# Bringing the experts' rows back amid the last expert's products, and turning rows behind the branch

## The reference, cut to what matters

```python
for l in range(2):
    h = x @ w_in[l]                       # 1892 columns; three kinds of attention follow
    x = layer_norm(ALPHA * x + mix @ w_out[l], ln1_g[l], ln1_b[l])
    x = layer_norm(ALPHA * x + moe_ffn(x, ...), ln2_g[l], ln2_b[l])

def moe_ffn(x, ...):                      # each row: one group of 4 experts, two experts in it
    h = silu(x @ w_gate[e]) * (x @ w_up[e]) * gates[:, e]
    return sum over e of h @ w_down[e]
```

## Time and profile before

| | |
|---|---|
| runs (us) | 1201.88, 1197.25, 1195.83 |
| median | 1197.25 us |
| profiled execution | 1202.57 us, of which the span is 1201.2 us |
| mean granted TensorE clock | 0.974 of full speed |
| TensorE busy | 1130.9 us (94%) |
| VectorE, ScalarE busy | 906.5 us (75%), 732.6 us (61%) |

### The profile page before, as it was taken

How to read it: one execution, slowest core, us unless ns; L and a number is a source line. 1 busy time by engine, 2 the same in 40 slices (tenths; PEclk the granted TensorE clock), 3 DMA queues, 4 the chain that set the end, 5 groups by cost and what they waited for, 6 DMA issues and landing times.

```text
span 1201.2 us, 14612 instructions
## 1 busy us (share of the span) xinstructions
PE 1130.9 (94%) x5487; PEld 927.0 (77%) x5487; DVE 906.5 (75%) x1482; ACT 732.6 (61%) x1307; POOL 0.2 (0%) x4
## 2 busy tenths in 40 slices
PE   3999999999998999998999999999989999999996
PEld 2788888788777788887788788877768878787774
DVE  3657666677666876776578767999986876899996
ACT  4545565654646665556355454888855655488883
POOL 0000000000000000000000000000000000000000
PEclk9999999999998999999999897999999999899999
DMA  9455353453332464622542323999936332399991
GB/s 303 140 210 175 106 178 138 167 183 106 140 117 95 140 224 161 222 105 85 196 144 103 105 71 113 336 359 366 366 122 210 129 106 71 126 338 357 366 352 40
DMA packets 131554, 221.26 MB, mean 184 GB/s; under 512 B 6112, under 2 KB 77328, under 8 KB 131472
## 3 DMA queue, kind: packets, MB, share of 16 engines
q1 hardware_dynamic: 126128, 209.60, 50.6%
q10 hardware_dynamic: 5344, 10.60, 2.7%
HBM read 219.13 MB, written 1.05 MB: 183 GB/s over the span
## 4 chain that ended last, share of the span: by engine, by line
PE 77%; DVE 11%; ACT 9%; issue 2%; DMA 1%; SPq 0%; DVEq 0%; ACTq 0%
PE bank L483 21%; PE bank L485 20%; PE bank L484 20%; PE bank L775 3%; PE bank L840 3%; ACT wH L428 2%; ACT S L795 2%; DVE wL L436 2%; PE bank L631 1%; DVE mx L784 1%; PE bank L821 1%; PE bank L2212 1%; PE bank L1756 1%; DMA M<-in_mem 1%; PE bank L1689 1%
## 5 line engine op out<-in xcount | busy, mean ns | idle before, releaser
L436 DVE TENSOR_TENSOR wL<-ring,wH 128x1024 fp32r<-128x1024 f32 (+1 forms) x316 | 375.0, 1212 | 142.9 <-ACT wH L428 142.1
L428 ACT ACTIVATE wH<-ring 128x1024 fp32r<-128x1024 f32 (+1 forms) x316 | 320.1, 1047 | 26.9 <-PE bank L485 15.4
L483 PE MATMUL bank<-wH,hTH 128*128 128x512 f32 (+2 forms) x592 | 238.3, 403 | 6.0 <-issue 3.2
L485 PE MATMUL bank<-wH,hTL 128*128 128x512 f32 (+2 forms) x592 | 232.2, 392 | 0.0
L484 PE MATMUL bank<-wL,hTH 128*128 128x512 f32 (+2 forms) x592 | 232.0, 392 | 0.0
L483 PEld LDWEIGHTS bank<-wH,hTH 128*128 128x128 f32 x592 | 112.2, 190 | 29.9 <-issue 5.8
L485 PEld LDWEIGHTS bank<-wH,hTL 128*128 128x128 f32 x592 | 112.0, 189 | 24.1
L484 PEld LDWEIGHTS bank<-wL,hTH 128*128 128x128 f32 x592 | 112.3, 190 | 22.4 <-issue 0.5
L483 PE MATMUL bank<-wH,xgH 128*128 128x512 f32 x256 | 104.8, 409 | 0.0
L485 PE MATMUL bank<-wH,xgL 128*128 128x512 f32 x256 | 101.1, 395 | 0.0
L484 PE MATMUL bank<-wL,xgH 128*128 128x512 f32 x256 | 100.9, 394 | 0.0
(11 more groups left out here) (292 smaller groups left out, 1898.3 us busy)
## 6 DMA issues: line engine op xcount, KB each, us to landing
ring<-in_w_in_a SPq DMA_DIRECT2D x44, 1024.0 KB, 4.9
ring<-in_w_out SPq DMA_DIRECT2D x20, 1024.0 KB, 4.8
ring<-in_w_down SPq DMA_DIRECT2D x20, 1024.0 KB, 5.8
ring<-in_w_gate SPq DMA_DIRECT2D x36, 512.0 KB, 4.9
ring<-in_w_up SPq DMA_DIRECT2D x36, 512.0 KB, 6.0
ring<-in_w_in_b SPq DMA_DIRECT2D x14, 1024.0 KB, 5.0
ring<-in_w_mem_kv SPq DMA_DIRECT2D x8, 1024.0 KB, 6.3
ring<-in_w_in SPq DMA_DIRECT2D x8, 1024.0 KB, 5.2
```

Source lines behind the costliest of these rows:

```text
L428: act.e.activation(quarter_parts(q)[0], quarter_in_ring(q), COPY).then_inc(w_high, 1)
L436: dve.e.tensor_tensor(lo, quarter_in_ring(q), hi.bitcast(F32), SUB).then_inc(w_low, 1)
L483: pe.e.matmul(o, a[0], b[0], start=first, stop=False)
L485: return pe.e.matmul(o, a[1], b[0], start=False, stop=last)
```

## The change

In the way "few", for both layers:

- `back(1, 0, 2)`, eight matmuls, now comes behind down(14), ahead of turned(15); it writes row tile 1's sums into two banks of `att_bank` in place of banks 2 and 3, and `dve_added` gets these banks as `sums_in`. The index of `att_bank` is set to 3 ahead of up(15), so up(15) takes bank 4, turned(14) bank 5, and the two sums banks 6 and 7.
- `back(1, 2, 3)`, four matmuls, comes behind down(15), ahead of back(0, 3, 4); `back(1, 3, 4)` comes last.

In layer 0, TensorE's turning of row tile 0 (8 transposes) is moved out of both ways of the branch, to the front of the next layer's code (`pe_flip_x(0, "exit", ...)`), on a semaphore `first_normed`. ScalarE's and VectorE's part of it stays in the branch.

In layer 1, VectorE's order is added 0, middle 0, added 1, middle 1, scaled 0, scaled 1, and the store is four transfers of 128 x 512 in place of two of 128 x 1024.

```diff
             for c, x in enumerate(in_two(X[:, i, :])):
                 mm = dve.e.scalar_tensor_tensor(x, in_two(middle[i])[c], r[:, 0:1], lnw[:, 1, c * 512:(c + 1) * 512], MUL, ADD)
-                if key[-1] == 0 and i == 1:
-                    mm.then_inc(second_normed, 1)
+                if key[-1] == 0:
+                    mm.then_inc((first_normed, second_normed)[i], 1)
...
+        def act_flip_exit(way):
+            for j0 in (0, 4):
+                act.wait_ge(at("turned", "xT", "exit", 0, j0))
+                act.e.activation(hT[0][:, j0:j0 + 4, 0:P], bank_of["xT", "exit", 0, j0].t[:, :].rearrange("p (j n) -> p j n", j=4),
+                                 COPY).then_inc(*act.did("high", "exit", way, j0))
+
+        def dve_flip_exit(way):
+            for j0 in (0, 4):
+                dve.wait_ge(at("high", "exit", way, j0))
+                dve.e.tensor_tensor(hT[1][:, j0:j0 + 4, 0:P], bank_of["xT", "exit", 0, j0].t[:, :].rearrange("p (j n) -> p j n", j=4),
+                                    hT[0][:, j0:j0 + 4, 0:P].bitcast(F32), SUB).then_inc(first_turned, 1)
...
         def pe_mix_layer(l):
+            if l:
+                turn["att"] = 3
+                pe_flip_x(0, "exit", X, [(first_normed, 1), (first_normed, 2)])
             second = [at("added", "o1", 1, c) if l == 0 else (second_normed, c + 1) for c in range(2)]
...
-        def pe_finish(l, way):
-            if l == 0:
-                pe_flip_x(0, way, X, [at("x", *way, 0, c) for c in range(2)])
...
-        def dve_finish(l, way, ready):
-            for i in range(2):
-                dve_added(i, way, ready[i])
+        def dve_finish(l, way, ready, sums_in=(None, None)):
+            for i in range(2):
+                dve_added(i, way, ready[i], sums_in[i])
                 dve_middle(i, way, ln_loaded(l, 2))
-                dve_scaled(i, way)
-                if l == 0 and i == 0:
-                    dve_flip_x(0, way)
+                if l == 0:
+                    dve_scaled(i, way)
+                    if i == 0:
+                        dve_flip_exit(way)
+            if l:
+                for i in range(2):
+                    dve_scaled(i, way)
 
         def sp_finish(l, way):
             if l == 1:
                 for i in range(2):
-                    sp.wait_ge(*[at("x", *way, i, c) for c in range(2)])
-                    sp.e.dma_start(out[0, i * P:(i + 1) * P, :], X[:, i, :]).then_inc(d_out, 16)
+                    for c in range(2):
+                        sp.wait_ge(at("x", *way, i, c))
+                        sp.e.dma_start(out[0, i * P:(i + 1) * P, c * 512:(c + 1) * 512], X[:, i, c * 512:(c + 1) * 512]).then_inc(d_out, 16)
...
                     if g0 == 0:
-                        pe.wait_ge(b.free, at(*way, "OHT", i))
-                        b.free = at("added", *way, i, n)
+                        if i:
+                            b = att_bank((*way, "back", 1, n), at("added", *way, i, n))
+                        else:
+                            b = bank_of[(*way, "back", 0, n)] = banks[n]
+                            pe.wait_ge(b.free)
+                            b.free = at("added", *way, i, n)
+                        pe.wait_ge(at(*way, "OHT", i))
...
             for e in range(16):
                 g = e // 4
+                if e == 15:
+                    turn["att"] = 3
...
                 if e == 14:
                     back(0, 0, 1)
+                if e == 15:
+                    back(1, 0, 2)
             turned(15)
             back(0, 1, 3)
             down(15)
+            back(1, 2, 3)
             back(0, 3, 4)
-            back(1, 0, 4)
-            pe_finish(l, way)
+            back(1, 3, 4)
```

More of the change, by code:

```diff
@@ L377, in program @@
     d_x0 = sem("d_x0")
-    first_turned, second_normed = sem("first_turned"), sem("second_normed")
+    first_normed, first_turned, second_normed = sem("first_normed"), sem("first_turned"), sem("second_normed")
     d_mem, d_ln, d_u, d_late = [sem(f"d_mem{i}") for i in range(2)], sem("d_ln"), sem("d_u"), sem("d_late")
@@ L1568, in in_two, with dve_added @@
             return [row[:, c * 512:(c + 1) * 512] for c in range(2)]
-        def dve_added(i, key, ready):
+        def dve_added(i, key, ready, sums_in=None):
             sums, mean = small(2, "sums", i, *key), small(1, "mean", i, *key)
@@ L1573, in dve_added @@
                 dve.wait_ge(ready[c])
-                dve.e.scalar_tensor_tensor(x, x, ALPHA, banks[2 * i + c].t[:, :], MUL, ADD, accum_out=sums[:, c:c + 1]).then_inc(*dve.did("added", *key, i, c))
+                dve.e.scalar_tensor_tensor(x, x, ALPHA, (sums_in or banks[2 * i:2 * i + 2])[c].t[:, :], MUL, ADD, accum_out=sums[:, c:c + 1]).then_inc(*dve.did("added", *key, i, c))
             dve.follow().tensor_scalar(mean, sums[:, 0:1], sums[:, 1:2], -1.0 / D, ADD, MUL).then_inc(*dve.did("mean", i, *key))
@@ L1602, in pe_flip_x @@
             for c, j0 in enumerate((0, 4)):
-                b = att_bank(("xT", name, i, j0), (first_turned, c + 1) if name in (("few", 0), ("all", 0)) else at("xT", name, i, j0))
+                b = att_bank(("xT", name, i, j0), (first_turned, c + 1) if name == "exit" else at("xT", name, i, j0))
                 pe.wait_ge(ready[c])
@@ L1619, in dve_flip_x @@
                 dve.e.tensor_tensor(hT[1][:, j0:j0 + 4, i * P:(i + 1) * P], bank_of["xT", name, i, j0].t[:, :].rearrange("p (j n) -> p j n", j=4),
-                                    hT[0][:, j0:j0 + 4, i * P:(i + 1) * P].bitcast(F32), SUB).then_inc(
-                    *((first_turned, 1) if name in (("few", 0), ("all", 0)) else dve.did("xT", name, i, j0)))
+                                    hT[0][:, j0:j0 + 4, i * P:(i + 1) * P].bitcast(F32), SUB).then_inc(*dve.did("xT", name, i, j0))
+        def act_flip_exit(way):
[8 more added lines that the diff above has]
+                                    hT[0][:, j0:j0 + 4, 0:P].bitcast(F32), SUB).then_inc(first_turned, 1)
         def dve_rotate(src, dst, n, w, c, s, *name, scratch=T0):
@@ L2186, in act_finish @@
                 if l == 0 and i == 0:
-                    act_flip_x(0, way)
-        def dve_finish(l, way, ready):
+                    act_flip_exit(way)
+        def dve_finish(l, way, ready, sums_in=(None, None)):
             for i in range(2):
-                dve_added(i, way, ready[i])
+                dve_added(i, way, ready[i], sums_in[i])
                 dve_middle(i, way, ln_loaded(l, 2))
-                dve_scaled(i, way)
-                if l == 0 and i == 0:
-                    dve_flip_x(0, way)
+                if l == 0:
[5 more added lines that the diff above has]
+                    dve_scaled(i, way)
         def sp_finish(l, way):
@@ L2246, in back @@
                 for n in range(2):
-                    b = banks[2 * i + n]
                     if g0 == 0:
-                        pe.wait_ge(b.free, at(*way, "OHT", i))
-                        b.free = at("added", *way, i, n)
+                        if i:
[5 more added lines that the diff above has]
+                        pe.wait_ge(at(*way, "OHT", i))
+                    b = bank_of[(*way, "back", i, n)]
                     for g in range(g0, g1):
@@ L2384, in dve_few @@
             down(15)
-            dve_finish(l, way, [[at(*way, "back", i, n) for n in range(2)] for i in range(2)])
+            dve_finish(l, way, [[at(*way, "back", i, n) for n in range(2)] for i in range(2)],
+                       [[bank_of[(*way, "back", i, n)] for n in range(2)] for i in range(2)])
         def experts(l):
@@ L2428, in write @@
             experts(l)
-        sp.wait_ge((d_out, 32))
+        sp.wait_ge((d_out, 64))
     def lanes(engines):
```

## The result

| | before | changed |
|---|---|---|
| median of 22 runs each (us) | 1198.70 | 1203.76 |
| lowest and highest | 1194.20, 1204.67 | 1196.49, 1209.71 |
| profiled execution's span | 1201.2 | 1201.7 |

The ratio changed to before is 1.0037, with a 95% interval of 1.0022 to 1.0052: 0.37% or 4.4 us slower (2.6 to 6.2). That is within the 0.5% bound and within the range of 1195.0 to 1205.0 us; it is 5 us above the 1198.7 that before had beside it. The profiled pair shows only 0.5 us between the spans, because the profiled execution of the changed kernel was already 2.8 us ahead when it came to the first changed place, in code that is the same. So I compare stretches: from VectorE's start on expert 15's hidden values in layer 0 to ScalarE's second copy of h10 (L551, tile 1), and from the same instruction in the last layer to the span's end.

A forecast was written before the change was run, and what follows sets the result against it. TensorE was taken as busy for 94% of the span, with 77% of the chain. Layer 0's +1.15 and the last layer's +0.85 gave +2.0 us on 1197.25, so 1199.3 us; range 1195.0 to 1205.0.

The forecast's parts named there:

- Part 1: back(1, 0, 2) ahead of turned(15): its eight matmuls delay down(15) by 1.6 us in layer 0, 1.85 in the last.
- Part 2: back(1, 2, 3) behind down(15): four matmuls, 0.93 us, in a 1.4 us TensorE gap; no cost, no gain.
- Part 3: Layer 0's transposes behind the branch: h10 starts 0.9 us earlier, then waits for the fourth quarter's split; layer 0 costs +1.15.
- Part 4: Last layer's VectorE order: shift of 1.85 us less 0.35 of waits for ScalarE's root, so +1.5 us.
- Part 5: Last layer's store by halves: less data behind the last half row, -0.65 us, bounds 0 and -0.9.
- the halved store gives nothing: Rival, chance 0.08: the last transfer's time is mostly not data; +2.65 us, 1199.9.
- A gain at the exit: Rival, chance 0.16: ScalarE's and VectorE's branch-exit stalls shrink, h10's start decides; layer 0 -0.85 us, total 1197.3.
- TensorE's exit is longer: Rival, chance 0.12: leaving layer 0's branch exceeds 3.24 us, delaying tile 0's transposes; +1.1 us, 1200.4.
- A half clock at the wrong time: Rival, chance 0.06: TensorE's half clock falls at 905, on h10's last k steps, for 17 us; +9.8, 1207.0.

The follow-up runs named there:

- e1: Kernel before with only the order of the bringing back (back matmuls) changed, transposes, last layer's order and store kept; ratio to before 1.0025.
- e3: Changed kernel with the fourth quarter of h10 split within the branch, beside down(15); ratio to before 1.0007.
- e2: Changed kernel with before's order of back matmuls, tile 1's sums sharing a bank with tile 0's turned rows, so overwritten; ratio to before 1.0016.
- e4: Kernel before with only the last layer's store in four transfers; ratio to before 0.9993.
- f3: Changed kernel with VectorE's last-layer order as before: added, middle, scaled of tile 0, then of tile 1; ratio to before 1.0051.
- f1: Changed kernel with both the order and the banks of the back matmuls as before; ratio to before 1.0005.
- k2: Changed kernel unaltered, timed a third time, beside before on another chip; ratio to before 1.0013.
- the combination: Kernel before plus transposes behind the branch, fourth quarter of h10 split within it and halved store, timed twice; ratios to before 1.0002 and 0.9996.
- f4: Changed kernel unaltered, timed again beside before on one chip; ratio to before 1.0047.
- f2: First timing of the combination (transposes behind the branch, early quarter split, halved store, else as before); ratio to before 1.0002.

## Why the prediction was right, point by point

It said 1199.3 us, no change beyond 0.5%, by a cost of 2.0 us. The ratio's 4.4 us has the sign that was forecast and lies within the bound; the size is twice that. The 2.1 us of the two stretches are near the forecast 2.0 partly by luck: in the last layer one term came out 0.6 us dearer and the next 0.4 us cheaper than they were put.

- **Part 1 (+1.6, +1.85).** Right: +1.62 and +1.85, and e1 shows that no other part is needed for them.
- **Part 2 (nothing).** Right: the four matmuls run in the gap; from down(15) to the first added it is 5.13 us in both kernels.
- **Part 3.** The sum is right (+1.05 to +1.08 for +1.15) and so is its reason: e3 took the fourth quarter's split away and 0.9 us went. One step was wrong without touching the sum: "with its 3.24 us it is out at 894.2" counted the way out from TensorE's last matmul. In these traces the branch instruction begins as the last matmul that waits is handed over (its weight load at 886.90 and the branch at 886.91 in the changed kernel, 888.54 and 888.62 in e2); in the changed kernel it ended 1.7 us ahead of the transposes, where the prediction had 0.4 us to spare. Had I used that step to reckon the transposes alone, as I did for e2, it would have said +1.9 where -0.6 came.
- **Part 4 (+1.5).** Mis-sized: -0.35 for the new order was +0.26. I priced the two roots at 0.8 us each from rows where VectorE works on them beside ScalarE. The trace of before has the very order of this change in each layer's first norm. There VectorE needs 2.37 us (layer 0) and 2.57 us (layer 1) from middle 1 to scaled 0; here it needed 2.72, and 2.57 in e3. Those were the nearer rows.
- **Part 5 (-0.65).** -1.06 in the pair, beyond its bound of -0.9, and the reason was wrong in part: less data behind the last half row should have given the same in every order, but e4 and f3 show 0.2 us with the order of before. The rest came only together with part 4's order, for a cause that stays open. In that order the rival "the halved store gives nothing" was the nearer one.
- **The rivals.** "A gain at the exit" did not come: ScalarE's 2.31 and VectorE's 1.55 us stayed. "TensorE's exit is longer" did not come either: the branch took 3.28 us (it did in e3, with 5.45). "A half clock at the wrong time" had 0.06; it is seen in one of three profiles of the changed kernel, just where it was put, at h10's last k steps, and in f1 at the same place; 8 of 46 runs are longer than any of before's. These 8 lie 6.7 us above the other 38, which is 8 / 46 x 6.7 = 1.2 us of the mean. Only one of the 8 has a profile (k2), so that all have its cause is not shown. It was priced as a case of its own, at 17 us of half clock; it should have been a term of the mean, for 3.4 us at that place (1.6 us) and the half clock that may follow in the next layer.
- **What stays open.** 2.1 us of stretches and about 1.2 us of long runs make 3.3, where the three comparisons at hand give 4.4, 5.5 and 2.6 (4.2 in the mean), and 2.9 to 3.5 at equal clock. What is left, 0.9 us of the mean, is no larger than what before shows against itself (1.1). Whether the low clock in the next layer's attention comes of the shifted times, or is met by chance, these profiles don't decide: it is in both of the combination, in one of three of the changed kernel, in none of the eight others.

The Trainium skill's page "TensorE: Matmul & The Clock Gate", section "HAM oscillation — how this bites in real kernels", has the clock fall after TensorE has stood idle. k2's and f1's rows fit that, with waits of 1.89 and 2.01 us for the fourth quarter just ahead of the fall or around it. A like wait can stand there without a fall: 1.80 us in e2, 1.78 in f3, 1.46 in f4, 1.33 in the changed kernel.

## What to carry to other kernels

Work moved from behind a wait to ahead of it must be priced where it then stands: eight matmuls that cost nothing beside VectorE's norm cost 1.85 us ahead of the last product, while the four put in a gap of 1.4 us cost nothing. When an engine starts earlier, look at once for the next thing that it needs from another engine; here 0.9 us of earlier start turned into a wait for a split, and that split had idle time to run in 17 us earlier. For effects of 2 us in 1200, compare stretches between the same instructions in two profiles, with the granted clock of each beside them: the mean of 12 runs moved by 1.1 us with nothing changed. And compare with the runs all the same, since e2, f2 and k3 had shorter stretches and no shorter runs.

## What the runs showed of the hardware that I had not expected

- TensorE's branch instruction at the exit took 3.28 to 3.72 us in ten profiles and 5.33 to 5.45 us in the three where the DMA engines were over half busy beside it. It ran while matmuls already handed over were still being worked off (e2), so it cost 3.24 us of idle time behind transposes that had waited for VectorE, and none that shows behind matmuls that wait for nothing more (e2, f1).
- ScalarE's branch instruction took 0.04 us in the changed kernel; its 2.40 us of idle time stood behind it.
- A mean granted clock lower by 0.001, that is 2.4 us of half clock, goes with 0.68 us more span. The places differ: in layer 0, 3.4 us of half clock on tile 0's last k steps and tile 1's first ones cost 1.6 us (k2) and 1.5 (f1 against e2). On tile 0's first 18 matmuls it cost the changed kernel nothing, since the wait for the fourth quarter stood behind: with 6.8 us there (changed) the last k steps began 25.33 us behind the hidden values, with 3.4 us (f3) 25.14.
- The last 256 KB of output took between 2.10 and 3.08 us to land, 512 KB 3.11 to 3.41.
- VectorE's L677 came 0.62 us after L673 in the last layer and 0.27 us after it one tile later, with ScalarE's value long there both times.
